# Recurrent heads: the latent values and the query as a fourth half-product pair, with a weight sum that waits for the gates only at its last step

## The reference

```python
pl = project(h_lat, w_in)                 # latent tokens, pl[0] query, pl[1], pl[2] forget gates,
pc = project(h_ctx, w_in)                 # pl[3] values, pl[4] output gate, pl[5..7] convolution
def hgrn_direction(q, z, v, lb, s0, reverse):
    log_f = jnp.logaddexp(jnp.log(lb), jnp.log1p(-lb) + jax.nn.log_sigmoid(z))
    k = (1.0 - lb) * jax.nn.sigmoid(-z)
    ...                                    # o_t = q_t s_t,  s_t = f_t s_(t-1) + k_t v_t
oc_f, sc_f = hgrn_direction(qc_h, z_c, i_c, lb_fwd, zero_state, False)   # context first
ol_f, _ = hgrn_direction(ql_h, z_l, i_l, lb_fwd, sc_f, False)            # then latent
a_lat = hgrn_readout(ol_f + ol_b, pl[4], hg_norm_g)
b_lat = pl[5] * depthwise_conv3(pl[6] * pl[7], conv_w)
```

## Time and profile before

| | us |
|---|---|
| median of 3 runs (lowest, highest) | 2822.43 (2818.26, 2822.80) |
| span of the profiled execution | 2814.1 |
| PE busy | 2697.8 (96%) |
| DVE busy | 1246.7 (44%) |
| ACT busy | 523.0 (19%) |
| POOL busy | 171.2 (6%) |

### The profile page before, as it was taken

How to read it: one execution, slowest core, us unless ns; L and a number is a source line. 1 busy time by engine, 2 the same in 40 slices (tenths; PEclk the granted TensorE clock), 3 DMA queues, 4 the chain that set the end, 5 groups by cost and what they waited for, 6 DMA issues and landing times.

```text
span 2814.1 us, 32083 instructions
## 1 busy us (share of the span) xinstructions
PE 2697.8 (96%) x12682; PEld 1796.7 (64%) x12682; DVE 1246.7 (44%) x2310; ACT 523.0 (19%) x870; POOL 171.2 (6%) x140
## 2 busy tenths in 40 slices
PE   7999999999899999999799999989999999999997
PEld 3688888887544444586344333334496877888886
DVE  4255656664444344535311111146573335654644
ACT  3122121222233233211100000022322113100001
POOL 1122211220000000132000000000000000000000
PEclk9999999999999999999899999999999999999999
DMA  9622111211111111225599999942102421233330
GB/s 346 212 60 57 54 52 45 60 30 38 38 53 53 45 53 49 79 75 183 231 409 409 409 409 409 409 154 64 42 1 83 125 77 46 78 87 90 90 90 30
DMA packets 327673, 374.57 MB, mean 133 GB/s; under 512 B 10033, under 2 KB 273030, under 8 KB 324230
## 3 DMA queue, kind: packets, MB, share of 16 engines
q1 hardware_dynamic: 327286, 371.93, 38.6%
q10 hardware_dynamic: 272, 1.05, 0.1%
HBM read 370.85 MB, written 2.10 MB: 133 GB/s over the span
## 4 chain that ended last, share of the span: by engine, by line
PE 91%; DVE 4%; DVEq 1%; DMA 1%; ACT 1%; issue 1%; SPq 0%; ACTq 0%
PE psum L1650 31%; PE psum L1952 12%; PE psum L1381 8%; PE psum L2108 6%; PE psum L720 3%; PE psum L1118 2%; PE psum L1837 2%; PE psum L815 2%; PE psum L728 2%; PE psum L2642 2%; PE psum L1878 2%; PE psum L705 2%; PE psum L1308 2%; PE psum L1360 2%; PE psum L1337 1%; PE psum L2724 1%
## 5 line engine op out<-in xcount | busy, mean ns | idle before, releaser
L1650 PE MATMUL psum<-arena 128*128 128x256 f32 x4144 | 907.9, 378 | 1.0 <-ACT arena L2740 0.5
L1650 PEld LDWEIGHTS psum<-arena 128*128 128x128 f32 x4144 | 779.2, 189 | 116.2 <-issue 5.3
L1952 PE MATMUL psum<-arena 128*64 128x512 f32 x1536 | 347.6, 597 | 3.0 <-issue 2.1
L1952 PEld LDWEIGHTS psum<-arena 128*64 128x64 f32 x1536 | 104.9, 136 | 217.5 <-issue 214.4
L1381 PE MATMUL psum<-arena 128*128 128x512 f32 x512 | 233.1, 597 | 0.0
L2108 PE MATMUL psum<-arena 128*128 128x512 f32 (+1 forms) x448 | 168.1, 532 | 0.0
L1682 DVE TENSOR_TENSOR arena<-psum,arena 128x256 f32<-128x256 f32 x66 | 28.0, 425 | 315.2 <-ACT arena L1695 192.6
L1381 PEld LDWEIGHTS psum<-arena 128*128 128x128 f32 x512 | 92.4, 189 | 104.1 <-issue 104.1
L1883 DVE SCALAR_TENSOR_TENSOR arena<-psum,arena 128x512 f32<-128x512 f32 x64 | 48.0, 750 | 246.4 <-PE psum L1878 245.8
L2108 PEld LDWEIGHTS psum<-arena 128*128 128x128 f32 x448 | 84.8, 190 | 80.8 <-issue 77.3
L1657 POOL TENSOR_TENSOR arena<-arena 128x512 f32<-128x512 f32 x34 | 48.2, 1418 | 1119.7 <-DMA arena<-in_w_in 653.3
(11 more groups left out here) (378 smaller groups left out, 3202.9 us busy)
## 6 DMA issues: line engine op xcount, KB each, us to landing
arena<-in_w_gate SPq DMA_DIRECT2D x64, 1024.0 KB, 18.3
arena<-in_w_up SPq DMA_DIRECT2D x64, 1024.0 KB, 16.2
arena<-in_w_down SPq DMA_DIRECT2D x64, 1024.0 KB, 18.0
arena<-in_w_in SPq DMA_DIRECT2D x120, 512.0 KB, 4.0
arena<-in_ada_w SPq DMA_DIRECT2D x24, 1024.0 KB, 7.4
arena<-in_w_up SPq DMA_DIRECT2D x32, 512.0 KB, 5.3
arena<-in_w_down SPq DMA_DIRECT2D x32, 512.0 KB, 4.8
arena<-in_w_out SPq DMA_DIRECT2D x16, 512.0 KB, 3.8
```

Of the source, the lines that this page charges most:

```text
L1650: mm = pe.matmul(psum[:, base + b, c * HALF:(c + 1) * HALF], w, v, start=(first and q == 0 and m in (0, 2, 3, 4)), stop=(last and q == KC ...
L1952: mm = pe.matmul(psum[64 * e:64 * e + 64, bank + n, :], tokens(e, 2 * q + k), w[:, k, 512 * n:512 * n + 512], start=(q == 0 and k == 0), s ...
```

## The change

The values of the latent tokens and the query become pair 3 (units 6 and 7). Only the two context tiles of the values stay plain, one after level 5 and one after pair 2. Since pair 3 leaves the latent values with channels on partitions, TensorE transposes them (`pe_turn_values`) and ACT copies them into `hw_v`. The query stays in `hq_o` and is read from there; its buffers and copies go, and level 0 of the next head moves to the end of the turn, ahead of the norm. The context gates are cut in two: the first stays behind pair 0, the second moves behind pair 1. POOL makes the sums of four pairs a head; those of pair 2 wait for the gates only ahead of the fourth operation. On VectorE, level 3 moves ahead of `dve_conv1`. ACT's order follows.

```diff
-            if g == 1 and not is_first(i):
-                done(pool, "hg", i - 1, 3)
+            if g == 1 and not is_first(i):
+                done(pool, "hg", i - 1, 7)
             if g == 2:
                 if not is_first(i):
                     done(pool, "hg", i, 1)
-                pool.wait_ge(sem("head_gates"), i + 1)
-            weight_sums(pool, *hg_pair(g), hg_sums(g), "hq_sums")
+            if g == 3:
+                done(pool, "hg", i, 3)
+            gates_read = lambda eng: eng.wait_ge(sem("head_gates"), i + 1)
+            weight_sums(pool, *hg_pair(g), hg_sums(g), "hq_sums", gates_read if g == 2 else None)
...
+        def pe_turn_values(pe, i):
+            pe.wait_ge(sem("hq_out"), i * 4)
+            for t in range(LT):
+                mm = pe.transpose(psum[:, 5, t * P:(t + 1) * P], hq_o[:, t * P:(t + 1) * P], ident)
+            mm.then_inc(sem("head_turned"), 1)
...
         def dve_begin(dve, i):
-            dve.wait_ge(sem("head_query"), i)
-            dve.tensor_copy(hw_q0, hp_q)
+            dve.wait_ge(sem("head_forget"), i)
             dve.tensor_tensor(hw_k0, hp_k[:, 0, C:T], hp_k[:, 1, C:T], ALU.add)
...
-                pe_level(pe, i, 0)
                 pe_hg_quad(pe, i, 0, levels({3: 1}))
-                pe_hg_gates(pe, i, lambda: pe_level(pe, i, 2))
+                pe_hg_gate(pe, i, 0)
+                pe_level(pe, i, 2)
                 pe_hg_quad(pe, i, 1, levels({1: 3, 3: 4}))
+                pe_hg_gate(pe, i, 1)
                 pe_level(pe, i, 5)
                 pe_hg_values(pe, i, 0)
                 pe_hg_quad(pe, i, 2, levels({1: 6, 3: 7}))
-                pe.wait_ge(sem("head_values_out"), i * 2 + 1)
+                pe_hg_values(pe, i, 1)
+                pe.wait_ge(sem("head_gates_out"), i + 1)
                 pe_turn_keys(pe, i)
-                pe_hg_values(pe, i, 1)
-                pe_states(pe, i)
...
-                pe_hg_query(pe, i, outputs)
+                pe_hg_quad(pe, i, 3, lambda pe, q: pe_states(pe, i) if q == 2 else None)
+                pe.wait_ge(sem("head_values_out"), i + 1)
+                pe_outputs(pe, i)
+                pe_turn_values(pe, i + 1)
+                pe_level(pe, i + 1, 0)
                 pe_head_norm(pe, i)
...
                 dve_level(dve, i, 2)
+                dve_level(dve, i, 3)
                 dve_conv1(dve, i)
-                dve_level(dve, i, 3)
                 dve_level(dve, i, 4)
...
                 dve_begin(dve, i + 1)
+                dve_hg_quad(dve, i, 3)
                 dve_readout(dve, i)
...
-        def weight_sums(eng, wa, wb, sums, formed):
+        def weight_sums(eng, wa, wb, sums, formed, last=None):
...
             eng.tensor_tensor(sums[1], sums[0], a[:, 0], ALU.subtract)
             eng.drain()
+            if last is not None:
+                last(eng)
             eng.tensor_tensor(sums[3], a[:, 1], sums[1], ALU.subtract)
```

More of the change, by code:

```diff
@@ L685, in pe_hg_quad @@
                 ws.arrived(pe, "hg", i, 2 * g + e)
[L686 to L689, removed]
+            pe.wait_ge(sem("hq_sums"), i * 4 + g)
+            pe.wait_ge(sem("hq_out"), i * 4 + g)
             pe_seven(pe, *hg_pair(g), hg_sums(g), HT[:, :, C:T], ht_t, 0, True, True, within)\
@@ L694, in gates_bank, with pe_hg_gate @@
             return 4 if is_first(i) else 6
-        def pe_hg_gates(pe, i, between):
-            if not is_first(i):
+        def pe_hg_gate(pe, i, d):
+            if d == 0 and not is_first(i):
                 pe.wait_ge(sem("head_out"), i)
[L700 to L709, removed]
@@ L711, in pe_hg_values @@
-        def pe_hg_values(pe, i, half):
-            if half == 0:
-                ws.arrived(pe, "hg", i, 6)
[L715 to L722, removed]
@@ L724, in pe_hg_query @@
-        def pe_hg_query(pe, i, within=None):
-            ws.arrived(pe, "hg", i, 7)
-            pe.wait_ge(sem("hq_out"), i * 3 + 3)
-            for k in range(KC):
[L728 to L731, removed]
+            ws.arrived(pe, "hg", i, 4 + d)
+            for k in range(KC):
+                if is_first(i) and d == 0:
+                    pe.wait_ge(sem("first_normed"), KC + k + 1)
+                mm = pe.matmul(psum[:, gates_bank(i), d * C:(d + 1) * C], ws.dst("hg", 4 + d)[:, k, :], HT[:, k, 0:C],
+                               start=(k == 0), stop=(k == KC - 1))
@@ new lines, in pe_hg_gate, with pe_hg_values @@
+            if d:
+                mm.then_inc(sem("head_gates"), 1)
+        def pe_hg_values(pe, i, t):
+            if t == 0:
+                ws.arrived(pe, "hg", i, 6)
+            for k in range(KC):
+                mm = pe.matmul(psum[:, 7, t * P:(t + 1) * P], HT[:, k, t * P:(t + 1) * P], ws.dst("hg", 6)[:, k, :],
+                               start=(k == 0), stop=(k == KC - 1))
+            if t == CT_ - 1:
+                mm.then_inc(sem("head_values"), 1)
+        def pe_turn_values(pe, i):
[3 more added lines that the diff above has]
+            mm.then_inc(sem("head_turned"), 1)
@@ L733, in act_hg_copy @@
         def act_hg_copy(act, i, g):
             done(act, "hg", i, 2 * g + 1)
-            if g:
+            if g == 0 and not is_first(i):
+                act.wait_ge(sem("head_taken"), i)
+            if g in (1, 2):
                 act.wait_ge(sem("hq_read"), i * 2 + g)
+            if g == 3:
+                act.wait_ge(sem("head_forget"), i + 1)
             if is_first(i) and g == 0:
@@ L803, in pe_level @@
             if l == 0:
-                pe.wait_ge(sem("head_begun"), i)
+                pe.wait_ge(sem("hq_out"), i * 4)
             else:
                 pe.wait_ge(sem("levels_out"), n)
+            if l == 1:
+                pe.wait_ge(sem("head_turned_out"), i)
             bank = psum[:, 4 + l % 2, :]
@@ L810, in pe_level @@
                 if l == 0:
-                    mm = pe.matmul(o, hw_k0[:, t * P:(t + 1) * P], hw_q0[:, t * P:(t + 1) * P], start=True, stop=True)
+                    mm = pe.matmul(o, hw_k0[:, t * P:(t + 1) * P], hp_q[:, t * P:(t + 1) * P], start=True, stop=True)
                 else:
@@ L940, in pe_hg @@
             late(0, 1)
-            pe_hg_gates(pe, 0, lambda: late(2, 3))
+            pe_hg_gate(pe, 0, 0)
+            late(2, 3)
+            pe_hg_gate(pe, 0, 1)
             late(4, 5)
@@ L946, in pe_hg, with turn_first @@
             pe_hg_values(pe, 0, 0)
-            late(10, 11)
-            pe_hg_quad(pe, 0, 2, lambda pe, q: late(12, 13) if q == 2 else None)
+            pe_hg_values(pe, 0, 1)
+            pe_hg_quad(pe, 0, 2, lambda pe, q: late(10, 11) if q == 2 else None)
+            late(12, 13)
             late(14, 15)
-            pe_hg_values(pe, 0, 1)
-            pe_hg_query(pe, 0)
-            pe.wait_ge(sem("head_values_out"), 2)
-            pe_mod_turn(pe, 1)
+            def turn_first(pe, q):
+                if q == 3:
+                    pe.wait_ge(sem("head_values_out"), 1)
+                    pe_mod_turn(pe, 1)
+            pe_hg_quad(pe, 0, 3, turn_first)
             pe_mod_turn(pe, 2)
+            pe_turn_values(pe, 1)
+            pe_level(pe, 1, 0)
             pe.wait_ge(sem("consts_in"), 32)
@@ L1011, in dve_hg @@
             dve_hg_quad(dve, 0, 2)
-            dve_mod_late(dve)
+            dve_mod_rows(dve, 1)
+            dve_mod_rows(dve, 2)
             dve_begin(dve, 1)
+            dve_mod_add(dve, 1)
+            dve.sem_inc(sem("mod_ready"), 1)
+            dve_hg_quad(dve, 0, 3)
+            dve_mod_last(dve)
             dve.wait_ge(sem("consts_in"), 32)
```

64 lines of the change are left out of this document (25 added, 39 removed).

## The result

The changed kernel takes 2847.76 us (median of 4 runs, 2847.11 to 2849.22), the kernel before 2822.61 (4 runs, 2818.26 to 2823.05): ratio 1.0091, 95% interval 1.0079 to 1.0104, so 25 us slower. Forecast were 2840, with 2828 to 2848 as the range: the sign is right, the size 8 us short, at the very edge of the range and beyond the 2834 to 2847 given for the case forecast. The profiled execution after has a span of 2845.0 in a run of 2847.11.

The account below looks back on a forecast made before the run. TensorE's work and waits bound the kernel (PE busy 96%). Seven turns +15.6, head 0 +1 and tail +0.9 make +17.5: span 2814.1 to 2831.6, on the runs' median 2840 us, range 2828 to 2848.

Parts of the forecast that it names:

- the case forecast: The prediction as worked out, with the new waits counted: 2840 us, own range 2834 to 2847, chance 0.70.
- Work and old waits: TensorE per head: work down 1.45 us, waits ahead of levels 0 and 5 gone (1.41), together -2.86 a turn.
- Level 1's copies and pair 1: GpSimd's sums of pair 2 hold VectorE's two copies, so TensorE waits 1.4 us ahead of pair 1; bounds 0 and 1.9.
- Level 5: VectorE's four multiplications take turns with GpSimd's sums, so level 6 on TensorE waits 2.0 us; bounds 0 and 3.5.
- Convolution: VectorE's convolution placed behind level 3 costs nothing.
- Tail: After the loop, the last norm is nearer to level 1, which already waits 0.90: +0.9 us, between 0 and 2.
- Rivals 1: VectorE's strided copies and broadcast multiplications are not held by GpSimd: about 2818 us, to 2814 at best; chance 0.09.
- 2 (the race falls the other way): GpSimd's first sum starts later, one VectorE copy or multiplication fewer is held: 2826 to 2833 us, chance 0.13.
- rival 3: TensorE's clock falls behind level 6's wait, some 2 us more a turn: 2854; chance 0.08, shared with a wait near its bound.
- The sum of the waits: New TensorE waits in a turn: 1.4 + 0.3 + 2.0 + 0.6 + 0.8 = 5.1 us; less 2.86, +2.2 a turn, seven times +15.6.
- Head 0: First head: less work and a shorter wait against late modulation weights, perhaps 3 us short ahead of pair 3: +1, between -3 and +4.
- the sum of a turn's waits: Rival set ahead of follow-up runs: all waits of a turn together make TensorE's clock fall; 2826 to 2831, 2831 to 2836, 2840 us.

Follow-up runs that it names:

- e3: Changed kernel with pair 2's first three sums held until VectorE is through level 3 and pair 3's sums until level 6: 2814.55 us, ratio 0.9973.
- e2: Changed kernel with the first three sums of pair 2 held back until VectorE is through level 3: 2835.27 us, ratio 1.0045.
- e1: Changed kernel with GpSimd's whole set of sums for pair 3 held back until VectorE is through level 6: 2824.67 us, ratio 1.0014.
- e7: Changed kernel with only the fourth sum of pair 3 held back until VectorE is through level 6: 2835.11 us, ratio 1.0048.
- e4: Changed kernel with VectorE's convolution back ahead of level 3: 2849.92 us, ratio 1.0098.
- e6: Kernel before, with only the fourth sum of pair 2 waiting for the gates: 2821.17 us, ratio 0.9995.
- e5: Changed kernel with all four sums of pair 2 waiting for the gates again: 2843.53 us, ratio 1.0077.

## Why the prediction was short

What held:

- *Work and old waits*: level 0 and level 5 wait for nothing now. e3's turn of 76.27 closes the account to 0.1.
- *Level 1's copies and pair 1*: 2.50 for the copies (forecast 2.5), pair 1's wait 1.5 from start to start (1.4). e2 removes it. The ends kept open, 0 and 1.9, can be dropped: the strided copy of 256 elements is held like the plain one.
- *Level 5*: level 6 late by 2.30 (2.0). e1 removes it, and e7 takes one operation's share of it, 0.9.
- *Convolution*: nothing, by e4. *Tail*: 1.81 for 0.90, as taken.
- Rivals 1 (the engines hardly meet) and 2 (the race falls the other way) are out: the first sum and the first copy stand in the order forecast.

The Trainium skill's "SBUF — State Buffer", section "Who interferes with whom", says that with a VectorE instruction in a two-port mode whoever issues first blocks the other for the whole instruction, and that an instruction with two SBUF inputs meets GpSimd's reads; the trace agrees, with 2.50 for 0.50 and 1.26 to 1.49 for 0.41 to 0.55. The recombination, with an input from PSUM, shows 0.43 beside a sum, as the same section has it.

What failed, in the order of size:

1. **The clock.** This is the step that failed, rival 3: the fall was kept out of the sum and held at 0.08, because "behind 2.07 the clock stayed" in one row of the kernel before. Behind level 6's 2.14 it fell in five turns of seven, at 1.7 each: 8.5 us. One wait that did not lower the clock was taken as showing that such waits don't. Two outcomes for one size of wait were possible, and seven draws of it were ahead; an expected share of them belonged in the sum, not beside it. The sign named for this rival, a granted clock below 0.98 in the loop, would have missed it too: the stretches with a fall read 0.98.
2. **The sum of the waits.** 5.1 a turn were forecast. From start to start they come to 1.5 + 0.4 + 2.3 + 0.6 + 0.6, and level 1 of pair 0 costs another 0.2, which I had not counted; unrounded that is 5.8. Without the falls the seven turns are +19.7 instead of +15.6, so 4.1. It is less than seven times 0.7 because the first turn of the kernel before had a stretch at lower clock of its own (42 records of pair 0 at 126.40 take 10.21, in the other turns 9.23). Transposes came 0.2 cheaper, level 6 0.3 dearer.
3. **Head 0.** Forecast +1, measured -0.8, so 1.8 in the other direction. The late modulation weights are waited for three times, 0.39 at 53.09, 1.95 at 60.70 and 3.39 at 107.33. The first two only use up the 2.5 us by which TensorE was ahead: its first 32 records of the section took 13.9 us (37.77 to 51.67) where before, in part at lower clock, they took 16.4 (37.93 to 54.37), and both kernels begin the second context gate at 61.7. The third costs 3.4 for the 3 put down. Against it, level 0's wait of 3.53 is one of 2.72 ahead of the transposes, level 0 runs at full clock behind it (0.9 in place of 1.7), and a wait of 0.48 at 120.57 is gone; 0.6 is left that I can't assign. The term is also no larger than its spread: the loop's pair 0 starts between 125.6 and 127.5 in the six kernels with this head 0, and at 126.4 and 127.2 in the two with the old one.

The third of these waits, and the one ahead of the transposes:

```profile
107.33 1.04 PE L438 MATMUL psum<-arena 128*2 128x512 f32 x8 [3.39 <-DMA arena<-in_ada_w]
...
124.25 0.66 PE L718 MATMUL psum<-arena 128*128 128x128 f32 x4 [2.72 <-DVEq L1692]
```

The three make 8.5 + 4.1 - 1.8 = 10.8. Between the spans the forecast, 2831.6, is 13.4 short of 2845.0; the tail has 0.2 of the rest and the stretch from the start of attention on 2.3, in two single executions, without a cause that I could show. Between the medians it is only 7.8 short, and that is luck: the 8.3 between span and median were read as what lies around a span. That is 2.1 (2847.11 for a span of 2845.0); the other 6 was the execution of the kernel before being quick, and the forecast added it to the changed kernel.

How little one row tells of the clock can be read from the tail, which is the same in the kernel before and in e6. First the kernel before, then e6, at the same waits (level 3 of the last head, its keys, its outputs; L1118 is a projection behind the keys):

```profile
692.31 1.23 PE L815 MATMUL psum<-arena 128*128 128x128 f32 x8 [2.02 <-DVEq L860]
...
731.75 7.03 PE L1118 MATMUL psum<-arena 128*128 128x512 f32 x16
...
745.14 0.49 PE L905 MATMUL psum<-arena 128*128 128x128 f32 x2 [2.48 <-DVEq L898]
```

```profile
694.09 1.88 PE L815 MATMUL psum<-arena 128*128 128x128 f32 x8 [2.01 <-DVEq L860]
...
733.97 1.31 PE L870 MATMUL psum<-arena 128*128 128x128 f32 x10 [2.07 <-DVEq L860]
735.11 8.73 PE L1118 MATMUL psum<-arena 128*128 128x512 f32 x16
```

Behind 2.02 the level takes 1.23, behind 2.01 it takes 1.88. Behind the 2.07 of the earlier trace rows the projection takes 7.03; behind the same 2.07 in e6 it takes 8.73, which is one fall of 1.7. And behind 2.48 the outputs fall to 0.64 a group from 746.50 on in the kernel before, a row of the same trace that the prediction did not use; behind 2.49 in e6 they stay at 0.39.

The cause of the slowdown is settled: GpSimd's first three sums of pair 2, and its last with the four of pair 3, stand beside two short stretches of VectorE on which TensorE waits. Through what the two engines hold each other up no run here shows by itself. What stays open is when the clock falls. By turns of seven: none behind waits of up to 1.4 (e1, e7, e3), two behind 2.30 (e2), four behind 2.49 (e5), five and seven behind 2.14 (the change and e4, with equal waits). So the size of the longest wait alone does not decide it. The counts go better with the sum of a turn's waits (from the second turn on), the rival put down ahead of e1, e2 and e7: none at 1.4 and 2.5 us (e3, e1), none and two at 3.7 (e7, e2), four at 4.0 (e5), five and seven at 4.6. It doesn't fix the count either, and no run was made to part the two. The moment plays a part: level 6 takes 1.93, 1.71 and 1.48 in the changed kernel's last three turns, and 2.00, 1.80, 1.60, 1.40 and 1.19 in turns two to six of e4, so the fall comes a little later against it from turn to turn. What it keeps step with was not tried.

## What to carry to other kernels

Where GpSimd and VectorE both work from SBUF, count, as here, one GpSimd operation of 1.1 to 1.3 us as 0.9 us lost for the one short VectorE instruction that meets it, and look for stretches where TensorE stands at the end of them; a wait on GpSimd that looks needless (here 0 us in the old order) may be what keeps the two apart. Placing the sums behind the levels made a slower kernel (+25 us) into a faster one (-7) with two waits and no change of work. When TensorE gets a new wait of about 2 us in a loop, put the fall of the clock into the sum with a share for each turn; here it was 18 turns of 28.

## What the runs showed of the hardware

- The clock fell behind waits of 2.14 to 2.49 us in 18 of the 28 turns of the four kernels with such a wait in the loop, at 1.3 to 1.7 us each. Equal instructions on TensorE and waits equal to 0.01 us (the change and e4) gave five and seven; waits of 2.0, 2.07 and 2.5 in the tail each had a fall in one execution and none in another (the kernel before and e6).
- GpSimd loses too: the second sum of a set, 1.27 alone, took 1.46 beside level 5 and 1.73 beside the convolution. In the turn above, the two engines took turns so strictly that a single VectorE instruction passed between two sums.
